# Expert weights in column steps of 512 and 1024, loaded in longer rows, and each unit rounded and subtracted in one instruction

## The reference, cut to what matters

```python
def swiglu(t, w_gate, w_up, w_down):
    return jnp.matmul(jax.nn.silu(jnp.matmul(t, w_gate)) * jnp.matmul(t, w_up), w_down)
...
for e in range(N_EXPERTS):
    y_e = swiglu(t, w_gate[e], w_up[e], w_down[e]).astype(jnp.float32)
    out = out + combine[:, e:e + 1] * y_e
```

## Time and profile before

| | |
|---|---|
| time, median of 3 runs | 1824.47 us (1824.45 to 1824.8) |
| span of the profiled execution | 1822.7 us |
| outside the span, against the median | 1.8 us |
| TensorE, matmuls | 1806.8 us busy (99%) |
| TensorE, weight loads | 1532.2 us (84%) |
| VectorE | 1500.1 us (82%) |
| ScalarE | 1265.1 us (69%) |
| GpSimd | 138.3 us (8%) |
| bytes moved | 512.49 MB, mean 281 GB/s |

### The profile page before, as it was taken

The page is one execution under the profiler, slowest core; times in us unless marked ns, Lnnn a source line. Parts: engine busy times, 40 slices in busy tenths (PEclk is TensorE's granted clock), DMA queues, the critical chain, the costliest instruction groups (busy, mean ns, idle before and its releaser), DMA issues.

```text
span 1822.7 us, 26908 instructions
## 1 busy us (share of the span) xinstructions
PE 1806.8 (99%) x9194; PEld 1532.2 (84%) x9194; DVE 1500.1 (82%) x1858; ACT 1265.1 (69%) x1660; POOL 138.3 (8%) x230
## 2 busy tenths in 40 slices
PE   9999999999999999999999999999999999999998
PEld 8888888888888899888888888888888888888886
DVE  6686787778666688586999999999999999999998
ACT  6645565556544666666878778787787777877876
POOL 2040050000000000140230000000000000000100
PEclk9999999999999999999999999999999999999999
DMA  9433568554555555515899999999999999999994
GB/s 338 153 95 138 177 189 338 196 196 139 188 194 174 171 176 185 185 38 171 334 377 397 406 367 384 391 351 411 376 370 390 360 404 371 368 405 362 384 412 183
DMA packets 239645, 512.49 MB, mean 281 GB/s; under 512 B 11036, under 2 KB 58490, under 8 KB 239498
## 3 DMA queue, kind: packets, MB, share of 16 engines
q1 hardware_dynamic: 235634, 493.08, 74.3%
q0 software_dynamic: 3808, 18.38, 2.5%
q10 hardware_dynamic: 144, 0.26, 0.0%
HBM read 505.38 MB, written 12.07 MB: 284 GB/s over the span
## 4 chain that ended last, share of the span: by engine, by line
PE 96%; DVE 2%; ACT 1%; issue 0%; POOL 0%; DVEq 0%; POOLq 0%; ACTq 0%
PE ps L262 25%; PE ps L264 25%; PE ps L263 25%; PE ps L2574 9%; PE ps L2577 4%; PE ps L2849 1%; PE ps L2369 1%; PE ps L2732 1%; DVE w_lo L255 0%; PE ps L2827 0%; PE ps L2292 0%; PE ps L2313 0%; PE ps L2689 0%; PE ps L2789 0%; PE ps L2246 0%
## 5 line engine op out<-in xcount | busy, mean ns | idle before, releaser
L255 DVE TENSOR_TENSOR w_lo<-raw,w_hi 128x1024 fp32r<-128x1024 f32 x937 | 1104.2, 1228 | 125.3 <-ACT w_hi L246 124.0
L246 ACT ACTIVATE w_hi<-raw 128x1024 fp32r<-128x1024 f32 x938 | 941.8, 1055 | 243.5 <-PE ps L264 230.6
L262 PE MATMUL ps<-w_hi,a 128*128 128x512 f32 (+1 forms) x1216 | 480.5, 395 | 0.8 <-DVE arena L1929 0.7
L264 PE MATMUL ps<-w_hi,a 128*128 128x512 f32 (+1 forms) x1216 | 472.7, 389 | 0.0
L263 PE MATMUL ps<-w_lo,a 128*128 128x512 f32 (+1 forms) x1216 | 471.7, 388 | 0.0
L262 PE MATMUL ps<-w_hi,a_hi 128*128 128x512 f32 (+1 forms) x720 | 280.6, 390 | 0.3 <-DVE a_lo L440 0.3
L264 PE MATMUL ps<-w_hi,a_lo 128*128 128x512 f32 (+1 forms) x720 | 278.7, 387 | 0.0
L263 PE MATMUL ps<-w_lo,a_hi 128*128 128x512 f32 (+1 forms) x720 | 278.6, 387 | 0.0
L264 PEld LDWEIGHTS ps<-w_hi,a 128*128 128x128 f32 x1216 | 228.2, 188 | 47.9
L262 PEld LDWEIGHTS ps<-w_hi,a 128*128 128x128 f32 x1216 | 228.5, 188 | 47.1 <-issue 1.7
L263 PEld LDWEIGHTS ps<-w_lo,a 128*128 128x128 f32 x1216 | 228.7, 188 | 44.3
(11 more groups left out here) (398 smaller groups left out, 1447.3 us busy)
## 6 DMA issues: line engine op xcount, KB each, us to landing
raw<-in_moe_w_gate_dram SPq DMA_DIRECT2D x112, 1024.0 KB, 6.9
raw<-in_moe_w_up_dram SPq DMA_DIRECT2D x112, 1024.0 KB, 7.3
raw<-in_moe_w_down_dram SPq DMA_DIRECT2D x112, 1024.0 KB, 7.1
raw<-in_ssd_w_in_dram SPq DMA_DIRECT2D x24, 1024.0 KB, 5.1
raw<-in_w_ffn_in_dram SPq DMA_DIRECT2D x22, 1024.0 KB, 5.1
raw<-in_w_in_dram SPq DMA_DIRECT2D x21, 1024.0 KB, 7.1
raw<-in_w_ffn_out_dram SPq DMA_DIRECT2D x11, 1024.0 KB, 4.9
raw<-in_dense_w_gate_dram SPq DMA_DIRECT2D x11, 1024.0 KB, 5.3
```

Source lines behind the costliest of these rows:

```text
L246: nc.scalar.activation(w_hi[:, u % SPL, part], raw[:, u % RAW, part], ACT.Copy).then_inc(hi_done, 1)
L255: last = nc.vector.tensor_tensor(w_lo[:, u % SPL, part], raw[:, u % RAW, part], w_hi[:, u % SPL, part].bitcast(F32), ALU.subtract)
L262: nc.tensor.matmul(o, lh, rh, start=start, stop=False, skip_group_check=True)
L264: return nc.tensor.matmul(o, ll, rh, start=False, stop=stop, skip_group_check=True)
```

## The change

- The 3584 inner columns are taken as one step of 512 and three of 1024 (`WIDE` holds the unit numbers at which gate, up and down of each wide step begin). A wide step has 4 units of gate into two banks, the transposes of the one or two products of the step before, 4 units of up into two banks, and then the down units of those products (2 in the first wide step, 4 in the second; in the third and at the end 8, with the transposes of the last two products between them). The 42 units, 504 matmuls and 28 product transposes of a task stay.
- Gate and up units of wide steps are 2 x 1024 columns (rows of 4 KB) in place of 4 x 512 (2 KB); a down unit holds two neighbouring rows for a partition (8 KB in one piece in place of two of 4 KB). To match it, `product` writes its result with the columns permuted: neighbouring results lie 128 elements apart.
- Units 6 to 43 of a task (42 and 43 are the next task's first two) are rounded by one ScalarE instruction of 2048 columns and subtracted by one VectorE instruction of 2048. Units 0 to 5 of task 0 and units 2 to 5 of the others stay in halves.
- `silu` and `product` come in pairs, `product_hi` and `product_lo` too, except in the first wide step.
- The inner loops of all engines are written out; a task's whole body is one pass of the outer loop.
- `row_add` comes twice behind a pair of products and twice behind a wide step. The tokens of the next task are transposed into banks 3 and 7, before down unit 36.

```diff
+HALVES = 7
+WIDE = ((4, 8, 22), (14, 18, 34), (26, 30, 38))
...
-        moe_down_v = I["moe_w_down_2"][0].rearrange("e (k p) n -> p e k n", p=P)
+        moe_down_v = I["moe_w_down_2"][0].rearrange("e (b p r) n -> p e b (r n)", p=P, r=2)
...
+            if u >= UNIT["moe"] + 6:
+                nc.scalar.activation(w_hi[:, u % SPL, :], raw[:, u % RAW, :], ACT.Copy).then_inc(hi_done, 2)
+                return
...
+            if u >= UNIT["moe"] + 6:
+                dve.wait_ge(hi_done, 2 * RAW * rounds + 2 * u + 2)
+                nc.vector.tensor_tensor(w_lo[:, u % SPL, :], raw[:, u % RAW, :], w_hi[:, u % SPL, :].bitcast(F32),
+                                        ALU.subtract).then_inc(lo_done, 1)
+                return
...
+                def silu(i, h, start=False):
+
+                    if h == 0:
+                        act.wait_ge(unit_used, used(M0 + 1, 7 * i))
+                    elif h % 2:
+                        act.wait_ge(unit_used, used(M0 + WIDE[h // 2][0] + 3, 7 * i))
+                    if not start or h > 1:
+                        act.wait_ge(m_mult, HALVES * i + h - 1)
+                    nc.scalar.activation(m_sg[:, h % 2, :], ps[GATE_BANK[h]][:, :], ACT.Silu).then_inc(m_silu, 1)
...
+                def wide_step(i, j, start=False):
+
+                    gate_u, up_u, down_u = WIDE[j]
+                    for u in range(gate_u + 2, up_u + 2):
+                        split_hi(act, M0 + u, 7 * i)
+                    silu(i, 2 * j + 1, start)
+                    silu(i, 2 * j + 2, start)
+                    for h in (0,) if j == 0 else (2 * j - 1, 2 * j):
+                        product_hi(i, h)
+                    for u in range(up_u + 2, WIDE[j + 1][0] + 2 if j < 2 else down_u - 2):
+                        split_hi(act, M0 + u, 7 * i)
...
-                    nc.vector.tensor_tensor(m_act, m_sg, ps[3][:, :], ALU.mult).then_inc(m_mult, 1)
+                    nc.vector.tensor_tensor(m_act[:, h % 2, :].rearrange("p (b r q) -> p b q r", b=2, r=2),
+                                            m_sg[:, h % 2, :].rearrange("p (b q r) -> p b q r", b=2, r=2),
+                                            ps[UP_BANK[h]][:, :].rearrange("p (b q r) -> p b q r", b=2, r=2),
+                                            ALU.mult).then_inc(m_mult, 1)
...
+                def wide_step_lo(i, j, added=None):
+
+                    gate_u, up_u, down_u = WIDE[j]
+                    for u in range(gate_u + 2, up_u + 2):
+                        split_lo(dve, M0 + u, 7 * i)
+                    for h in (0,) if j == 0 else (2 * j - 1, 2 * j):
+                        product_lo(i, h)
+                    for u in range(up_u + 2, up_u + 6):
+                        split_lo(dve, M0 + u, 7 * i)
+                    product(i, 2 * j + 1)
+                    product(i, 2 * j + 2)
+                    if added:
+                        added()
+                    for u in range(up_u + 6, WIDE[j + 1][0] + 2 if j < 2 else down_u - 2):
+                        split_lo(dve, M0 + u, 7 * i)
...
+                wide_step_lo(0, 0)
                 positions()
+                wide_step_lo(0, 1)
...
+                wide_step_lo(n_last, 0, lambda: row_add(0, 0))
+                row_add(0, 1)
+                wide_step_lo(n_last, 1, lambda: row_add(1, 0))
+                row_add(1, 1)
+                wide_step_lo(n_last, 2)
...
+                    pe.wait_ge(m_silu, HALVES * i + 1)
+                    wide(4, (2, 3), 7 * i)
+                    turn_product(i, 0)
+                    wide(8, (6, 7), 7 * i)
+                    down_block(i, 12, 0, 0, True)
+                    down_block(i, 13, 0, 1)
+                    pe.wait_ge(m_silu, HALVES * i + 3)
+                    wide(14, (2, 3), 7 * i)
+                    turn_product(i, 1)
+                    turn_product(i, 2)
+                    wide(18, (6, 7), 7 * i)
+                    for q in range(4):
+                        down_block(i, 22 + q, 1 + q // 2, q % 2)
...
+                    down_block(i, 34, 3, 0)
+                    turn_product(i, 5)
+                    turn_product(i, 6)
+                    down_block(i, 35, 3, 1)
+                    if more:
+                        turn_rows(i)
+                    down_block(i, 36, 4, 0)
```

More of the change, by code:

```diff
@@ L856, in task_loads, with rows_of, down @@
                 def task_loads(expert, i):
[L858 to L875, removed]
+                    def rows_of(u, src, k0, n, cols):
+                        moe_load(u, src[:, expert, k0:k0 + n, cols].rearrange("p a k n -> p (a k) n"), 7 * i)
+                    def down(u, block):
+                        moe_load(u, moe_down_v[:, expert, block:block + 1, :].rearrange("p a k n -> p (a k) n"), 7 * i)
+                    for half in range(2):
+                        rows_of(half, moe_gate_v, 4 * half, 4, slice(0, WB))
+                    for half in range(2):
+                        rows_of(2 + half, moe_up_v, 4 * half, 4, slice(0, WB))
+                    for j, (gate_u, up_u, down_u) in enumerate(WIDE):
+                        cols = slice(WB + j * D, WB + (j + 1) * D)
+                        for q in range(4):
+                            rows_of(gate_u + q, moe_gate_v, 2 * q, 2, cols)
+                        for q in range(4):
+                            rows_of(up_u + q, moe_up_v, 2 * q, 2, cols)
+                        first = 0 if j == 0 else 4 * j - 2
+                        for q in range(first, 4 * j + 2):
+                            down(12 + q if j == 0 else WIDE[j - 1][2] + q - first, q)
+                    for q in range(4):
+                        down(38 + q, 10 + q)
                 task_loads(slice(0, 1), 0)
@@ L1382, in task_end_hi, with task_hi @@
                                              ACT.Copy, scale=m_gate).then_inc(m_yhi, 1)
[L1384 to L1391, removed]
+                def task_hi(i, more):
+                    for j in range(3):
+                        wide_step(i, j)
+                    task_end_hi(i, more)
                 first_hi()
@@ L2123, in row_add @@
                     C.link(nc.vector.tensor_tensor(x[:, t, :], x[:, t, :], y_back[n][t], ALU.add))
-                def step_lo(n):
-                    split_lo(dve, M0, n)
-                    split_lo(dve, M0 + 1, n)
-                    product_lo(n - 1)
-                    for u in range(2, 6):
-                        split_lo(dve, M0 + u, n)
-                    product(n, used(M0 + 1, n))
-                def task_lo(i, more):
-                    with dve.Fori(1, 6) as j:
-                        step_lo(7 * i + j)
-                    task_end_lo(i, more)
```

251 lines of the change are left out of this document (122 added, 129 removed).

## The result

The changed kernel takes **1855.05 us** (median of 4 runs, 1853.61 to 1856.07) against 1824.48 in the runs beside it: ratio 1.0164, 95% interval 1.0152 to 1.0177. The forecast was 1833.5, range 1824 to 1845. The sign was right, the size was not.

A forecast was written before the change was run, and what follows sets the result against it. TensorE's matmuls, busy for 99% of the span, were taken as the bound. Late units 4.3, last task 3.0 and first task 1.7 sum to 9.0 us; span 1822.7 + 9.0 = 1831.7, plus 1.8 outside: 1833.5 us, range 1824 to 1845.

The forecast's parts named there:

- 0.54 a task: Units 10, 20 and 32 of each task come 0.16, 0.19 and 0.19 us late; 4.3 us for 8 tasks.
- So 0.68 us for 512 columns at the bottom, twice that at the top; I take 0.68: VectorE's product, writing neighbouring results 512 bytes apart, was taken at 0.68 us, from a 256-column row.
- the dear product: Rival: the strided product takes 1.36 us, making units 14, 24 and the third pair's transposes late, 1862 us; 9%.
- the 0.17 to spare: With two products ahead of VectorE's subtraction, units 14 and 24 were to be ready 0.17 us early, at no cost.
- The long instruction's lead: VectorE starts only when all 2048 columns are rounded; a unit's plain margin falls from 1.63 to 0.84 us.
- Last task: Last task: two row_adds 1.18 us late each, two 0.3 together, last unit 0.52 against 0.18; 3.0 us together.
- Task 0: In the first task, positions, table loads and GpSimd's multiplies add 1.7 us, between 0.5 and 3.
- Transfers: A weight buffer is free for 12.1 us and a transfer lands in 6.9, so transfers cost 0.
- Code loading: Rival: TensorE's longer loop body doesn't stay on chip, six jumps back wait for code, 20 us more, 1854; 8%.
- Cheaper matmuls: Rival: longer rows in the DMA queues make TensorE's matmuls, 0.227 us apart, cheaper, by 56 us at most; 5%.
- The order of units: TensorE's same 504 matmuls and 36 transposes a task in another order, costed at nothing.

The follow-up runs named there:

- experiment 1: The changed kernel with the product written contiguously and the down weights in their old row order (two rows of 4 KB): 1834.63 us, ratio 1.0055.
- experiment 3: The changed kernel with the same permutation, but the product written in line and both sources read in steps of 8 bytes: 1834.97 us, ratio 1.0059.
- experiment 4: The changed kernel with every unit rounded and subtracted in halves of 1024 columns, the scattered product kept: 1827.77 us, ratio 1.0018.
- experiment 5: The changed kernel with halves for every unit, a contiguous product and the old row order of the down weights: 1824.86 us, ratio 1.0001.
- experiment 7: The kernel before with long 2048-column instructions alone for expert units, order and transfers as before; only units 0 to 5 of task 0 left out: 1826.81 us, ratio 1.0013.
- experiment 11: The changed kernel without the four row_adds, so the other tasks' results are missing from the output: 1852.18 us in one run.
- experiment 9: The changed kernel with VectorE's subtraction alone in halves for units 22 to 35 of task 0: 1850.57 us, median of two runs.
- experiment 10: The changed kernel with ScalarE's rounding alone in halves for units 22 to 35 of task 0: 1850.53 us, median of two runs.
- experiment 8: The changed kernel with units 22 to 35 of task 0 in halves on both ScalarE and VectorE: 1849.5 us.
- experiment 6: The changed kernel with halves, contiguous product, old down row order, and each row_add and positions behind one more subtraction: 1823.33 us, ratio 0.9994.

## Why the forecast was right in sign and wrong in size

The span's growth, from the starts of the tasks in each trace. Before 1822.7, experiment 1 1833.2, after 1853.6 us:

| | forecast | experiment 1 | after |
|---|---|---|---|
| ahead of task 0 | 0 | 0.14 | 0.35 |
| task 0 | 2.2 | 1.8 | 8.6 |
| six middle tasks | 3.2 | 4.3 | 15.8 |
| last task | 3.5 | 4.1 | 6.1 |
| sum | 9.0 | 10.4 | 30.9 |

(The forecast's 0.54 a task is counted with each task.)

**The step that failed** is "So 0.68 us for 512 columns at the bottom, twice that at the top; I take 0.68". The product took 1.095. The nearest row was a test of reads and writes with steps of 8 bytes inside short runs, and I let it stand for writes that go by turns to two places 512 bytes apart. The prediction's own sign of being wrong, a product over 0.8 us, came true. The Trainium skill ("Advanced Engine Details and Errata", SBUF Cachelines) had the direction: experiments 1 and 3 show the penalty that it speaks of, 0.415 us for 512 writes, and experiment 3 shows none for reads in steps of 8 bytes, which that rule, taking two hits on a line as enough, would also allow. I quoted it and gave the dear product 9%. The price was neither of the two I had, but in between.

**How 0.4 us became 20.** The pair at unit 14 holds the subtraction for 0.67 longer; less the 0.17 to spare that is 0.50, and 0.59 was measured, at units 14 and 24. The third pair had 0.10 to spare and lost 0.57. Together 1.75 of the 1.88 us between the middle tasks of experiment 1 and of the kernel after. Of the 20.4 us between the two spans the six middle tasks have 11.5, task 0 has 6.8 and the last task 2.0. The same product costs a middle task nothing with halves (experiment 4). The two parts multiply: against the kernel of experiment 5 the long instructions cost 9.8 us, the scattered product 2.9, both together 30.2.

**The long instruction's lead** held. Unit 10 was late by 0.15 (0.16 forecast), units 20 and 32 by 0.30 and 0.31 (0.19 each), more than half as much again. That the middle task still came near the forecast is in part luck: the order of the units gave 0.15 back, which the forecast had at nothing. Without the dear product the middle task was 119.23 against the 119.0 of the text. That it costs only where something stands ahead of it is shown by experiment 7: the old order with the same instructions loses nothing in the six middle tasks, and task 0 is 0.4 us longer.

**Last task.** Two `row_add` at 1.18 each behind a pair of products: 1.26 in experiment 1; with the dear product 1.95, and 0.59 without them (experiment 11), so 1.36 for each, the whole length of one.

**Task 0.** 1.8 us in experiment 1, with the 1.7 and the 0.54 against it. But in the kernel after 8.6, and about 4.4 of that (the difference to experiments 9 and 10) is a path I never followed: GpSimd's indirect transfers, whose result TensorE needs 38 us later. The text named GpSimd's multiplies and not its DMAs. Before, the gather was issued at 952.45, its rows landed 7.4 us later, and TensorE turned them at 970.84: 11.0 us to spare. In the kernel after it was issued 10.3 us later: GpSimd reached its slot rows 2.9 us later, needed 6.2 longer until it read them back, and 1.2 longer from there. Landing took 2.9 us more (10.3), and the rows were wanted 0.6 sooner. Together 13.8 us against 11.0, and the clock then charged extra for the gap.

**Transfers** at no cost: right. Landing takes 7.0, 7.6 and 7.0 us for gate, up and down weights, and experiment 5, with all of the wider loads of gate and up, is level with before. But one reading was wrong: ScalarE's wait of 1.6 us for gate weights lay not at the stage's start but in the last task:

```profile
1720.10 2.01 ACT L246 ACTIVATE w_hi<-raw 128x1024 fp32r<-128x1024 f32 x2 [1.60 <-DMA raw<-in_moe_w_gate_dram]
```

So the slack reckoned for transfers did not hold there even before the change; experiments 7 and 8 have such waits again. **Code loading**, 8%: it did not come. Over 1020 to 1740 us the instruction queues of the kernel after moved

```profile
q14 instruction: 3, 0.02, 0.0%
```

though a pass on TensorE is now some 1080 instructions long. TensorE shows no gap in experiment 4, which has the same loop (118.34 us busy in a middle task of 118.34). The Trainium skill's rule ("Runtime: NRT & Kernel Launch", Instruction fetch mechanics) that a jump outside a two-block window must fetch isn't borne out by this loop; its figure of 2048 instructions is not contradicted. **Cheaper matmuls**, 5%: the spacing is 0.227 us in every kernel, whatever the length of the rows.

**The order of units** at nothing: nearly. A middle task is 118.34 in experiments 4 to 6, against 118.49 before and in 7. The transposes are the same in number; in three places of a task two groups now stand next to each other. That this is what saves the 0.15 was not tried by itself.

## What to carry to other kernels

Count the margin before the parts: where a chain has 0.17 us to spare in 6, an operation whose price no row shows decides the case, and it is worth measuring or avoiding. Here the permutation could have stood on the reading side for nothing (experiment 3). Merging two instructions into one saves their fixed cost on an engine that may be idle anyway, and takes away the head start of whoever reads the first half; with single short pieces ahead of it that is free, with pairs it isn't. And a long instruction on one engine can hold up an engine that shares no data with it; follow GpSimd's transfers to the one who needs them.

## What was not expected of the hardware

- VectorE writing 512 float32 results by turns into two rows 512 bytes apart takes 1.095 us; in line it takes 0.680, also when both sources are read in steps of 8 bytes.
- GpSimd's indirect transfer of slot rows took 7.40 us beside long instructions on VectorE and ScalarE, and the same 7.40 in the run without `row_add`; 2.99 with ScalarE in halves, 1.91 with VectorE in halves or both, 1.77 before. With a contiguous product and long instructions on both (experiment 1) the first took 2.30. The transfer of 7.40 us began 0.2 us into three subtractions that ran without a gap:

```profile
932.27 6.68 DVE L259 TENSOR_TENSOR w_lo<-raw,w_hi 128x2048 fp32r<-128x2048 f32 x3
939.72 2.29 DVE L259 TENSOR_TENSOR w_lo<-raw,w_hi 128x2048 fp32r<-128x2048 f32 x1 [0.76 <-ACT w_hi L247]
```

  and ended at 939.88, 0.9 us behind them and 0.2 us into the next one. The Trainium skill ("SBUF — State Buffer", SBUF: two separate sides) says that a VectorE instruction with two SBUF inputs and a GpSimd operation that reads SBUF lock each other out of a shared port pair for a whole instruction. The row agrees with it as far as it goes; no run here shows whether this transfer counts as such an operation. But in 10 the transfer began as early in three such subtractions and took 2.99 us, in experiment 1 it began 0.9 us into them and took 2.30, and in experiment 7, where the units around it are long on both engines too, it began 1.8 us into two of them and took 1.66. So a lock alone doesn't explain when it strikes, nor what ScalarE has to do with it; that stays open.
- After 3 us of idle TensorE's granted clock fell to the 1.2 GHz level for 3.4 us, and in experiment 8 after a wait of 2.2 us for 3.4 again. In the last task of the kernel after it stood idle for 1.7 us and stayed at 2.4 GHz (1.00):

```profile
1758.00:1760.50 2.50, 1.08 (x5) 0.91 (x6) 2.50 (x2) 1.75 (x1) 0.00 (x0) 1.00 1.03 421
```

  So of two waits that differ by half a microsecond one can cost its own length and the other 1.6 us more: the eight matmuls behind the gap took 3.52 us from start to start in experiment 8 (1753.48 to 1757.00) and 1.95 us in the kernel after.
- A transpose's weight load from columns 8 bytes apart takes 205 ns, against 141.
